# Weight splits moved ahead in the block-product loop, and weight places that restart in each FFN stage

## The reference, cut to what matters

```python
def swiglu(x, wi, wo):
    g, u = jnp.split(x @ wi, 2, axis=-1)
    return (jax.nn.silu(g) * u) @ wo

def ffn_half(x, g_pre, g_post, wi, wo):
    return x + 0.5 * rmsnorm(swiglu(rmsnorm(x, g_pre), wi, wo), g_post)
```

## Time and profile before

| what | value |
|---|---|
| median of 3 runs | 2272.39 us (2266.97 to 2278.84) |
| the profiled execution's own time | 2267.56 us |
| its span | 2265.9 us |
| PE matmul busy | 2056.4 us, 91% |
| DVE busy | 1458.0 us, 64% |
| ACT busy | 841.1 us, 37% |
| POOL busy | 599.3 us, 26% |
| HBM traffic | 87 GB/s over the span |
| granted TensorE clock, mean | 0.963 |

### The profile page before, as it was taken

How to read it: one execution, slowest core, us unless ns; L and a number is a source line. 1 busy time by engine, 2 the same in 40 slices (tenths; PEclk the granted TensorE clock), 3 DMA queues, 4 the chain that set the end, 5 groups by cost and what they waited for, 6 DMA issues and landing times.

```text
span 2265.9 us, 37860 instructions
## 1 busy us (share of the span) xinstructions
PE 2056.4 (91%) x16328; PEld 2019.1 (89%) x16328; DVE 1458.0 (64%) x1991; ACT 841.1 (37%) x1066; POOL 599.3 (26%) x491
## 2 busy tenths in 40 slices
PE   9798988999999698988998898988999989898799
PEld 9798988999899698988998798978999989898799
DVE  7746466856768656466785646464897874646567
ACT  5423233423444323233452323233486432323343
POOL 0246163032200137164000244371000013616300
PEclk9899999999999899989999899999999989999999
DMA  4322222145412222222222223122222321222222
GB/s 145 101 70 93 72 83 103 57 153 161 157 43 108 73 68 82 87 84 93 84 94 75 75 75 111 59 86 81 75 95 77 112 85 56 86 83 84 93 84 76
DMA packets 95302, 202.79 MB, mean 89 GB/s; under 512 B 6144, under 2 KB 74016, under 8 KB 85664
## 3 DMA queue, kind: packets, MB, share of 16 engines
q1 hardware_dynamic: 89424, 183.55, 23.7%
q0 software_dynamic: 5424, 16.50, 2.4%
q10 hardware_dynamic: 288, 0.32, 0.0%
HBM read 193.78 MB, written 4.48 MB: 87 GB/s over the span
## 4 chain that ended last, share of the span: by engine, by line
PE 65%; DVE 26%; ACT 4%; issue 4%; DMA 2%; POOL 0%; DVEq 0%; ACTq 0%; POOLq 0%
PE acc L2120 29%; PE acc L2289 24%; PE acc L2230 8%; DVE w_lo L1285 6%; DVE spare_lo L1285 3%; DVE hid_lo L1644 2%; DMA raw<-in_weights 2%; DVE t L1398 2%; DVE x L1405 1%; DVE act_lo L1411 1%; ACT w_hi L841 1%; DVE gu L1666 1%; DVE rs_post L1393 1%; DVE act_lo L1587 1%; PE acc L2351 1%
## 5 line engine op out<-in xcount | busy, mean ns | idle before, releaser
L1285 DVE TENSOR_TENSOR w_lo<-raw,w_hi 128x1792 fp32r<-128x1792 f32 (+3 forms) x204 | 436.6, 2140 | 103.7 <-ACT w_hi L841 103.6
L841 ACT ACTIVATE w_hi<-raw 128x1792 fp32r<-128x1792 f32 (+3 forms) x204 | 347.6, 1721 | 207.5 <-POOL raw L696 132.8
L690 POOL TENSOR_TENSOR raw<-raw 128x512 f32<-128x512 f32 x99 | 158.9, 1605 | 647.6 <-DMA raw<-in_weights 647.6
L2289 PE MATMUL acc<-act_hi,w_hi 128*128 128x260 f32 x990 | 201.9, 285 | 6.5 <-DVE act_lo L1587 6.5
L991 ACT ACTIVATE gu<-acc 128x260 f32<-128x260 f32 x66 | 25.5, 386 | 477.6 <-PE acc L2289 477.6
L2289 PE MATMUL acc<-act_hi,w_lo 128*128 128x260 f32 x990 | 200.9, 285 | 0.0
L2289 PE MATMUL acc<-act_lo,w_hi 128*128 128x260 f32 x990 | 200.7, 285 | 0.0
L2120 PE MATMUL acc<-act_hi,w_hi 128*128 128x260 f32 (+1 forms) x960 | 196.6, 286 | 0.0
L2120 PE MATMUL acc<-act_hi,w_lo 128*128 128x260 f32 (+1 forms) x960 | 193.4, 283 | 0.0
L2120 PE MATMUL acc<-act_lo,w_hi 128*128 128x260 f32 (+1 forms) x960 | 193.0, 283 | 0.0
L1658 DVE TENSOR_TENSOR t<-acc,gu 128x260 f32<-128x260 f32 x66 | 28.3, 429 | 255.5 <-ACT gu L991 255.5
(11 more groups left out here) (378 smaller groups left out, 5360.5 us busy)
## 6 DMA issues: line engine op xcount, KB each, us to landing
raw<-in_weights SPq DMA_DIRECT2D x72, 1024.0 KB, 4.8
raw<-in_weights SPq DMA_DIRECT2D x103, 512.0 KB, 3.7
raw<-in_weights SPq DMA_DIRECT2D x24, 896.0 KB, 4.5
spare_raw<-in_weights SPq DMA_DIRECT2D x33, 512.0 KB, 3.7
spare_raw<-in_weights SPq DMA_DIRECT2D x8, 896.0 KB, 4.5
ring<-in_k_pages POOLq DMA_DIRECT2D x16, 256.0 KB, 3.6
raw<-in_weights SPq DMA_DIRECT2D x12, 256.0 KB, 5.7
out_y<-x SPq DMA_DIRECT2D x8, 260.0 KB, 2.1
```

The costliest lines, as they stand in the source:

```text
L690: nc.gpsimd.tensor_tensor(pairs(quad(n, 4, 2)), pairs(quad(n, 1, 2)), quad(n, 3).unsqueeze(1).broadcast_to([P, 2, QUAD]), ALU.add)\
L841: nc.scalar.activation(w_hi[n][:, at:size], raw(n, size)[:, at:size], ACT.Copy).then_inc(hi_ready, 1)
L1285: nc.vector.tensor_tensor(w_lo[n][:, at:size], raw(n, size)[:, at:size], w_hi[n][:, at:size].bitcast(F32), ALU.subtract).then_inc(lo_ready, 1)
L2289: ins = nc.tensor.matmul(out, w[n + h][:, at * QUAD + i * P:at * QUAD + (i + 1) * P], m[:, i, :], start=h == 0 and k == 0 and i == 0, stop ...
```

## The change

Three things are edited. In the plan, each FFN stage sets the turn of the sums places to zero, so that its first sums go to the spare buffer; it lets one plain place go by, if the last plain unit of the stage would otherwise lie at 0 (this happens in stage 6 alone); and ahead of the output weights it sets the turn of the plain places to 2 (stages 0 and 4: place 4096) or 0 (stages 2 and 6: place 0). On ACT, the high part of the hidden tile before and the first split of the next pair's weights go ahead of the wait for block b and its copy. On DVE, the low part of the pair's own second weights, the low part of the hidden tile before and the low part of the next pair's first weights go ahead of the sum of block b, in this order.

```diff
     def ffn(s, name, layer):
         w = (name + "_wi", layer)
+        pl.turns[SUMS] = 0
+        if (pl.turns[UNIT] + FIRST_SUM(s) - 1) % 3 == 0:
+            pl.turns[UNIT] += 1
         for a, b in PHASES:
...
+        pl.turns[UNIT] = 0 if s % 4 else 2
         out_pairs(s, (name + "_wo", layer), PHASES[-1][0])
...
             def sum_hidden(s, j, previous):          # ACT
                 g = gu_of(s, j)[:, 0, :]
-                wait_job(act, f"{s}.b{j}")
-                nc.scalar.activation(cols(g, 0), acc_of(f"{s}.b{j}")[:, 0, 0:HALF], ACT.Copy).then_inc(one_copied, 1)
                 if previous:
                     sum_hid_hi(s, j - 1)
                 n = U[f"{s}.sums{j}.0"] + 2
                 split(n)
+                wait_job(act, f"{s}.b{j}")
+                nc.scalar.activation(cols(g, 0), acc_of(f"{s}.b{j}")[:, 0, 0:HALF], ACT.Copy).then_inc(one_copied, 1)
                 if is_sums(n):
                     split(n + 1)
                 wait_drained(act, f"{s}.c{j}")
...
                 if previous:                         # DVE
                     last_sums(s, j - 1)
-                if previous:
                     sum_product(s, j - 1)
+                    split_low(n - 1)
+                    sum_low(s, j - 1)
+                split_low(n)
                 dve.wait_ge(one_copied, pairs_count(n - 2))
                 drains(nc.vector.tensor_tensor(u2, b[:, 1, :], cols(g, 0), ALU.add), f"{s}.b{j}")
...
-                if previous:
-                    sum_low(s, j - 1)
                 dve.wait_ge(dve_order, mark)
...
-                split_low(n)
                 wait_job(dve, f"{s}.c{j}")
...
-                if is_sums(n):
-                    split_low(n + 1)
```

## The result

The changed kernel takes 2068.78 us (median of 4 runs, 2067.05 to 2070.6), the kernel before 2275.35 beside it (4 runs): ratio 0.9097, 95% interval 0.9069 to 0.9126. That is 206.6 us less. The forecast was 2100, its range 2070 to 2165: the sign was right and so was the mechanism in the main, the gain was larger than the range allowed, by little.

The account below looks back on a forecast made before the run. PE sets the end, losing time standing for low weight splits queued late and at low clock. Gains of 65.5 + 83.6 + 27.4 - 6 = 170.5 off 2267.6 give 2097, as a median run 2100 us; range 2070 to 2165.

Parts of the forecast that it names:

- the rest of 0.5 us that each pair was to keep: Block products: each pair keeps 0 to 0.9 us of PE's standing, 0.5 taken; 12 us and 14 us off the gains.
- 8-pair phases: Four phases of 8 pairs, 430.00 us: 96 gained, less 12.4 for waits ahead of out0, so 83.6.
- the meeting of DVE and POOL: In each pair, DVE's steps with two SBUF operands and POOL's sums wait each other out: 2.7 us on top for DVE.
- the sign named for a rest: Sign of being right: a 7-pair phase lasts some 73 to 75 us at clock 0.98 or more.
- Out0 waits: Ahead of the first output weights: 4 to 5 us of waiting in stages 2 and 6, none in 0 and 4.
- First pairs and phases: First sums go to the spare place: stage 2 gains 8.6, stage 4 10.8, second pairs 4 each; together 27.4 us.
- The skipped turn: Start of stage 6: in0's later place costs 4 us of standing and about 1.7 of low clock; 6 lost.
- the shared port sets the pair: Rival: DVE and POOL exclude each other, 10.9 us a pair, 21 us more, 2121; chance 0.20.
- POOL (2162 to 2225): Rival: both sets of POOL's sums stretched, 12.9 us a pair, 2225, half of that 2162; chance 0.10.
- ACT's fixed order: Rival, slower: ACT's first split waits for POOL's sums with b's copy behind it; 2300 at 10.4 us; chance 0.04.
- A wait that only changes its name: Rival: PE stands for claims instead, and pairs and skip eat what the places give; 2270; chance 0.03.
- No rest: Better than forecast: pairs keep no standing and the skip in stage 6 is hidden; about 2070; chance 0.08.

Follow-up runs that it names:

- the kernel with the last places: Changed kernel without the skipped place, and two sums places passed over within the first phase's output weights in stages 2 and 6: 2054.14 us, ratio 0.9022.
- the order-alone kernel: Changed kernel with the new order on ACT and DVE but the weight places as before the change: 2100.91 us, ratio 0.9238.
- the kernel without POOL's reads: Changed kernel with POOL's three sums per weight load replaced by memsets that read nothing, so weight sums are left out: 2053.0 us, ratio 0.9024.
- half of the order: Changed kernel with the new order on DVE only, ACT in the old order, new places kept: 2253.84 us, ratio 0.9915.
- the kernel without the skip: Changed kernel without the skipped plain place in stage 6: 2065.89 us, ratio 0.9068.

## Why the forecast came out too high

The profiled executions differ by 2267.56 - 2070.6 = 197.0 us; the forecast had 170.5. Term by term:

- **The step that failed: the rest of 0.5 us that each pair was to keep** (12 us for the 7-pair phases, 14 for the 8-pair phases: 26 us). The prediction found the meeting of DVE and POOL, sized DVE's lateness at up to 0.9 us a pair, and then booked its middle as time of PE. Measured: 7-pair phases 282.54 us, with POOL's reads gone 282.43; 8-pair phases 333.16 and 332.14. So the rest is 1.1 us in 60 pairs. Against it stand some 5.5 us that the forecast had at nothing: a pair of 84 matmuls takes 10.09 us with nothing in its way, not 10.0. Net, the step makes 19 of the 26.5 us that were missed. In the 7-pair phases the gain was 357.49 - 282.54 = 74.95, forecast 65.5, and the sign named for a rest, phases of 73 to 75 us, was missing: they took 70.6 to 70.7.
- **Why the rest was nothing.** The prediction had the numbers: second weights ready at 4.8, wanted at 5.0; the next ones at 8.9, wanted at 10.0; and "b, a and c then end 0.9 us later than PE would like". What PE would like is no deadline. b's accumulator is claimed only by the next pair, and b's sum, at 173.08, was in time for that at 174.78. A lag that is in time at every deadline costs 0; the 0.5 was the middle of two bounds, where the prediction's own numbers at the two edges gave the lower one.
- **How much the meeting cost DVE** was too high as well: 2.7 us a pair in the forecast, 1.3 measured (36.13 us in 28 pairs). That is part of why the lateness, after a first step of some 0.5 us, grew by some 0.08 us a pair and not by 0.9.
- **Where luck comes in.** The prediction has nothing of lateness that carries over from pair to pair. Its deadline was reached in the seventh or eighth pair, and the phases have 7 and 8. Pairs at the edge took 10.15 to 10.17 us; from that, an estimate for longer phases is a rest of some 0.07 us a pair. No run has such phases.
- **8-pair phases**: 430.00 - 333.16 = 96.84 gained, forecast 83.6. 32 x 10.0 and 9.04 us of standing ahead of out0 leave 4.1 us, where 14 were forecast: 9.9 of the 13.2 missed. The other 3.4 is the low clock behind the two out0 waits, which the forecast put into these phases and which lies behind them: 11 and 10 steps of two matmuls took 4.89 and 4.43 us there, at 0.24 a step otherwise, so 4.3 us were lost.
- **Out0 waits**: stages 2 and 6 alone, 4.53 and 4.51 us; forecast 4.5 in those two and none in 0 and 4. Right, and the kernel with the last places shows that they stood on the path: without them the phases lose 8.7 us.
- **First pairs and phases**: idle and length together 10.8 + 21.35 became 1.95 + 20.52 in stage 2 (9.7, forecast 8.6), 10.8 + 37.48 became 30.84 in stage 4 (17.4 with its second pair, forecast 14.8 with 4 of it), stages 0 and 6 nearly unchanged (the prediction took stage 6's first wait of 1.32 us for stage 0 too; it was 1.57, and is 2.65 and 3.39 us now). About 27.6 in all, forecast 27.4. The order by itself took none of the 10.8, as the order-alone kernel shows.
- **The skipped turn**: 3.40 us of standing at 1620 and some 1.5 us of low clock behind it (two matmuls in 0.64 us from 1621.75 on, against 0.40; the eight steps from 1621.36 to 1624.78 take 3.42 us in place of 1.92): 4.9 us, forecast 6 (the expectation above put 5.6). The wait was right in place, and nearly in size.
- 74.95 + 96.84 + 27.6 - 4.9 is 194.5; the other 2.5 us of the 197.0 were not placed.

The rivals: that the shared port sets the pair (2121), or POOL (2162 to 2225), fell with pairs of 10.09 us and with the kernel without POOL's reads. The 10.9 us a pair of the first of them counts POOL's sums at their whole length; in the trace they shut DVE out for less, and its own counterargument held (the last section has the numbers). ACT's fixed order (2300) did not come up: the split ahead of the copy, at 167.61, waits for nothing, and the one behind it waits 2.07 us for POOL and is in time. Only in the two pairs of stage 2 shown above did ACT's order, with POOL's sums late, cost 0.4 and 0.3 us. A wait that only changes its name is what half of the order gives (2253.84), not the whole. "No rest" had 0.08 in the forecast, together with a hidden skip. The skip was paid and no rest was left, and the low end of the range was drawn at the sum that needed both.

## What to carry to other kernels

When an engine off the path gets later, write down for each of its results when the bounding engine takes it, and book only what is late at that point. Lateness short of that point is free, and the middle between two bounds is no estimate when the deadlines can be read. Then ask whether the lateness carries over, how fast it grows and what wipes it out: here it came up to the deadline just as the phases ended. Last, ask how much slack is left: one more sum of 0.42 us a pair was nearly free and 1.4 us cost 80 us. A reorder of a buffer that one engine hands to another pays only when both engines are reordered.

## What the runs showed of the hardware

- POOL's 128x256 sum, 0.73 us with DVE elsewhere, took 2.40 us beside a DVE split, and the split 2.56 in place of 2.01 in that same pair; with POOL only filling, every 128x1792 split took 2.01 to 2.03 us.
- The two engines shut each other out for less than the length of POOL's sums. In the changed kernel a low hidden tile that met the 128x512 sum took 1.1 us more (40 of 66 of them, 1.78 to 1.80 for 0.69), and a split that met a 128x256 sum 0.55 more (2.56 for 2.01), while these sums take 1.28 and 0.73 us by themselves. Two sets of sums then shut DVE out for 2 x (1.1 + 2 x 0.55) = 4.4 us a pair, an estimate; with DVE's own 5.5 that is 9.9, below PE's 10.09.
- Waits that come often and are short left the clock alone: with DVE's new order by itself PE stood for 131 us in waits of 1.1 and 1.7 us on average, and three of its four 7-pair phases still ran at a granted clock of 1.00 (the fourth at 0.96, the 8-pair phases at 0.94 to 1.00). The fall does not always come with the wait: after the 3.40 us at 1620 the first matmuls ran at full speed, and the slow ones, at the lower level of 1.2 GHz, began 1.3 us later; after the 4.53 us ahead of 978.23 the first matmuls were slow already.
- The first phase of stage 4 took 30.8 us in two executions of the changed kernel and 33.6 in the kernel without the skip, which is the same up to stage 6. Differences of 3 us in one profiled execution's first phases say nothing; that POOL meets DVE differently there is likely, not shown.
